# One more place in the weight ring for four of the eight expert turns

## The reference, cut to what matters

```python
def swiglu(h, w_gu, w_down):
    g, u = jnp.split(h @ w_gu, 2, axis=-1)
    return (jax.nn.silu(g) * u) @ w_down

def moe_swiglu(h, w_router, b_router, w_gu, w_down):
    tok = h.reshape(B * S, D)
    logits = tok @ w_router + b_router
    top_v, top_i = lax.top_k(logits, TOP_K)
    gates = jax.nn.softmax(top_v, axis=-1)
    combine = jnp.sum(jax.nn.one_hot(top_i, N_EXPERTS) * gates[..., None], axis=1)
    for e in range(N_EXPERTS):
        out = out + combine[:, e:e + 1] * swiglu(tok, w_gu[e], w_down[e])
    return out
```

## Time and profile before

| | |
|---|---|
| time, median of 3 runs | 1353.53 us (1351.11 to 1354.9) |
| profiled execution, its own time | 1350.77 us |
| span in the profile | 1349.0 us |
| PE, PEld busy | 96%, 75% |
| DVE, ACT busy | 63%, 48% |
| queue q1 (SP's transfers) | 393.68 MB, 76.0% of the 16 DMA engines' span |

### The profile page before, as it was taken

The page is one execution under the profiler, slowest core; times in us unless marked ns, Lnnn a source line. Parts: engine busy times, 40 slices in busy tenths (PEclk is TensorE's granted clock), DMA queues, the critical chain, the costliest instruction groups (busy, mean ns, idle before and its releaser), DMA issues.

```text
span 1349.0 us, 18058 instructions
## 1 busy us (share of the span) xinstructions
PE 1296.4 (96%) x7339; PEld 1012.9 (75%) x7339; DVE 843.6 (63%) x899; ACT 652.3 (48%) x675; POOL 86.3 (6%) x118
## 2 busy tenths in 40 slices
PE   9999999999999999999999997999979999799987
PEld 8999998888888999999888534885348863388632
DVE  6998876555555999876788304883038830388421
ACT  6545664554444454665576204762037630376401
POOL 1003000000000002100174000000000000000100
PEclk9999999999999999999999998999989999899999
DMA  9555964555554654653899999999999999999996
GB/s 314 186 194 198 337 225 162 176 189 190 188 189 143 206 188 141 218 170 123 349 403 391 386 423 424 423 422 401 423 424 423 417 385 424 424 423 419 386 423 284
DMA packets 127855, 411.89 MB, mean 305 GB/s; under 512 B 7422, under 2 KB 76382, under 8 KB 100638
## 3 DMA queue, kind: packets, MB, share of 16 engines
q1 hardware_dynamic: 121838, 393.68, 76.0%
q0 software_dynamic: 3408, 12.85, 2.5%
q10 hardware_dynamic: 2528, 4.23, 0.9%
HBM read 396.31 MB, written 14.42 MB: 304 GB/s over the span
## 4 chain that ended last, share of the span: by engine, by line
PE 83%; DMA 6%; issue 5%; ACT 3%; DVE 2%; POOL 0%; ACTq 0%; POOLq 0%; DVEq 0%; SPq 0%
PE bank L1938 23%; PE bank L1940 23%; PE bank L1939 23%; PE bank L2428 9%; DMA arena<-in_w_moe_gu 3%; DMA arena<-in_w_moe_down 2%; ACT WH L1282 1%; DVE WL L1853 1%; PE bank L2489 1%; PE bank L1982 0%; DMA xs<-in_x 0%; DMA xrows<-ysb 0%; PE bank L2359 0%; PE bank L2101 0%; PE bank L2109 0%
## 5 line engine op out<-in xcount | busy, mean ns | idle before, releaser
L1853 DVE TENSOR_TENSOR WL<-arena,WH 128x2048 fp32r<-128x2048 f32 x129 | 294.8, 2291 | 84.5 <-ACT WH L1282 84.2
L1359 DVE TENSOR_TENSOR WL<-arena,WH 128x2048 fp32r<-128x2048 f32 x108 | 245.2, 2272 | 92.8 <-ACT WH L961 92.7
L1938 PE MATMUL bank<-WH,XH 128*128 128x512 f32 (+1 forms) x728 | 274.9, 378 | 21.7 <-DVE WL L1853 21.7
L1282 ACT ACTIVATE WH<-arena 128x2048 fp32r<-128x2048 f32 x129 | 247.1, 1921 | 96.7 <-PE bank L1940 83.8
L1939 PE MATMUL bank<-WL,XH 128*128 128x512 f32 (+1 forms) x728 | 271.8, 373 | 0.0
L1940 PE MATMUL bank<-WH,XL 128*128 128x512 f32 (+1 forms) x728 | 271.1, 372 | 0.0
L961 ACT ACTIVATE WH<-arena 128x2048 fp32r<-128x2048 f32 x109 | 206.3, 1894 | 75.4 <-PE bank L1940 62.2
L1938 PEld LDWEIGHTS bank<-WH,XH 128*128 128x128 f32 x728 | 139.3, 191 | 48.7 <-DVE WL L1853 16.5
L1938 PE MATMUL bank<-XH,WH 128*128 128x256 f32 x592 | 168.1, 284 | 0.4 <-DVE XL L1389 0.4
L1940 PE MATMUL bank<-XH,WL 128*128 128x256 f32 x592 | 167.5, 283 | 0.0
L1939 PE MATMUL bank<-XL,WH 128*128 128x256 f32 x592 | 167.5, 283 | 0.0
(11 more groups left out here) (348 smaller groups left out, 1559.7 us busy)
## 6 DMA issues: line engine op xcount, KB each, us to landing
arena<-in_w_moe_gu SPq DMA_DIRECT2D x128, 1408.0 KB, 13.8
arena<-in_w_moe_down SPq DMA_DIRECT2D x84, 1024.0 KB, 16.4
arena<-in_w_in SPq DMA_DIRECT2D x27, 1024.0 KB, 5.1
arena<-in_w_ffn_gu SPq DMA_DIRECT2D x44, 512.0 KB, 4.8
arena<-in_w_xkv SPq DMA_DIRECT2D x16, 1024.0 KB, 5.3
arena<-in_w_ffn_down SPq DMA_DIRECT2D x11, 1024.0 KB, 5.0
xrows<-hTl POOLq DMA_DIRECT2D x8, 1024.0 KB, 9.1
arena<-in_w_mix_out SPq DMA_DIRECT2D x8, 1024.0 KB, 8.6
```

Of the source, the lines that this page charges most:

```text
L1282: a.activation(WH[:, (NA + i) % HL, :], raw[i % RING_M], ACT.Copy).then_inc(hi_ready, 1)
L1359: v.tensor_tensor(WL[:, n % HL, 0:w], s[:, 0:w], WH[:, n % HL, 0:w].bitcast(F32), ALU.subtract).then_inc(lo_ready, 1)
L1853: v.tensor_tensor(WL[:, (NA + i) % HL, :], raw[i % RING_M], WH[:, (NA + i) % HL, :].bitcast(F32), ALU.subtract).then_inc(lo_ready, 1)
L1938: te.matmul(out, ah, bh, start=start, stop=False, skip_group_check=shared)
```

## The change

The back half of that home, 2048 floats per partition, becomes `spare`, a twelfth unit, used in light turns alone. `early0` and `early1` move to the first third of `WH`. In a light turn the first 2048 columns of the gate lap go to `spare` and the rest to `arena` from its start; the up lap starts in `arena` unit 10, goes on in `spare` and then in `arena`; the down units 0, 1, 2 go to units 9, 10 and `spare`, the later ones to `raw[u - 3]`. Rows that cross a place's end are loaded and multiplied in pieces. `load_turn` is left with heavy turns alone.

```diff
-        WH = sb("WH", [P, HL, UNIT], F32R)
+        WH, early0, early1 = share([("WH", [P, HL, UNIT], F32R)], [("early0", [P, D], F32), ("early1", [P, D], F32)])
...
-        MH, ML, hThm, hTlm, early0, early1, hTf, xT = share(
+        MH, ML, hThm, hTlm, spare, hTf, xT = share(
             [("MH", [P, KC * S], F32R), ("ML", [P, KC * S], F32R)],
-            [("hThm", [P, D], F32R), ("hTlm", [P, D], F32R), ("early0", [P, D], F32), ("early1", [P, D], F32)],
+            [("hThm", [P, D], F32R), ("hTlm", [P, D], F32R), ("spare", [P, UNIT], F32)],
...
+        spare_landed, slot_landed = sem("spare_landed"), sem("slot_landed")
+        LIGHT_DOWN_SEM = (8, 9, 10, 0, 1, 2, 3, 4, 5, 6, 7)
+        LIGHT_DOWN_ROW = [None, 0, 1] + [(u * UNIT - 1) // FF for u in range(3, RING_M)]
...
+        def light_place(stage, c):
+            if c < UNIT:
+                return (spare, c) if stage == 0 else (arena, 10 * UNIT + c)
+            if stage == 0:
+                return arena, c - UNIT
+            return (spare, c - UNIT) if c < 2 * UNIT else (arena, c - 2 * UNIT)
...
+        def light_unit(u):
+            return spare[:, :] if u == 2 else raw[9 + u if u < 2 else u - 3]
...
+            def load_light_turn(e, turn, nth, last=False):
+                def heavy_down(u):
+                    floor = 0 if isinstance(turn, int) else LOOP_FROM // 2 * NM
+                    sp.wait_ge(lo_ready, heavy(turn, NM, max(NA - RING_M + u + 1, floor)))
+
+                load_light_row(e, 0, 0, 0, UNIT, spare_landed)
+                heavy_down(0)
+                load_light_row(e, 0, 0, UNIT, FF, part_landed[0])
+                for r in range(1, KC):
+                    heavy_down((r * FF + FF - UNIT - 1) // UNIT)
+                    load_light_row(e, 0, r, 0, FF, part_landed[r])
+                heavy_down(RING_M - 1)
+                load_light_row(e, 1, 0, 0, UNIT, slot_landed)
+                sp.wait_ge(*light_through(0, 0, nth))
+                load_light_row(e, 1, 0, UNIT, FF, part_landed[0])
+                sp.wait_ge(*light_through(0, 1, nth))
+                load_light_row(e, 1, 1, 0, 2 * UNIT - FF, part_landed[1])
+                load_light_row(e, 1, 1, 2 * UNIT - FF, FF, part_landed[1])
+                for r in range(2, KC):
+                    sp.wait_ge(*light_through(0, r, nth))
+                    load_light_row(e, 1, r, 0, FF, part_landed[r])
...
+                for u in range(RING_M):
+                    if u:
+                        sp.wait_ge(*light_through(1, LIGHT_DOWN_ROW[u], nth))
+                    load_light_down(e, u)
...
-                    if isinstance(turn, int):
-                        down_used(turn - 1, row_end(r))
...
+                    sp.wait_ge(*light_through(2, min(row_end(r) + 3, RING_M - 1), LIGHT.index(
+                        (turn if isinstance(turn, int) else LOOP_FROM) - 1)))
...
-                        pe.wait_ge(*row_in(stage, r, turn))
-                        for j, (o, w) in enumerate(SEGS):
...
+                        if r == 0:
+                            pe.wait_ge(slot_landed if stage else spare_landed, 16 * nth + 16)
+                        pe.wait_ge(*light_row_in(stage, r, turn, nth))
+                        for j, a0, w in light_pieces(stage, r):
...
-                    w = raw[u]
+                    w = light_unit(u)
```

More of the change, by code:

```diff
@@ L619, in gathered, with light_cols, light_pieces @@
             return bank[GATHER_BANK[b]][:, :].rearrange("p (c s) -> p c s", c=2)[:, :, 0:P]
+        def light_place(stage, c):
[4 more added lines that the diff above has]
+            return (spare, c - UNIT) if c < 2 * UNIT else (arena, c - 2 * UNIT)
+        def light_cols(stage, c, w):
+            tile, at = light_place(stage, c)
+            last_tile, last = light_place(stage, c + w - 1)
+            assert tile is last_tile and last == at + w - 1
+            return tile[:, at:at + w]
+        def light_unit(u):
+            return spare[:, :] if u == 2 else raw[9 + u if u < 2 else u - 3]
+        def light_pieces(stage, r):
+            pieces = []
+            for j, (o, w) in enumerate(SEGS):
+                cuts = {0, w}
+                for start in (r * FF + o, r * FF + FF // 2 + o):
+                    for edge in ((UNIT,), (UNIT, 2 * UNIT))[stage]:
+                        if start < edge < start + w:
+                            cuts.add(edge - start)
+                cuts = sorted(cuts)
+                pieces += [(j, a, b - a) for a, b in zip(cuts, cuts[1:])]
+            return pieces
         def heavy_sg(j):
@@ L668, in load_row, with load_down, load_light_row @@
                 sp.dma_start(arena[:, r * FF:r * FF + FF], src).then_inc(part_landed[r], 16)
-            def load_down(e, u, light):
+            def load_down(e, u):
+                src = w_moe_down[0][bass.ds(e, 1), u * 256:u * 256 + 256].rearrange("o (p k) n -> (o p) (k n)", k=2)
+                sp.dma_start(raw[u], src).then_inc(part_landed[DOWN_SEM[u]], 16)
+            def load_light_row(e, stage, r, c0, c1, landed):
+                w = w_moe_gu[0].rearrange("e (k p) (s f) -> e k s p f", p=P, s=2)
+                src = w[bass.ds(e, 1), r, stage, :, c0:c1].rearrange("o p f -> (o p) f")
+                sp.dma_start(light_cols(stage, r * FF + c0, c1 - c0), src).then_inc(landed, 16)
@@ L671, in load_down, with load_light_down @@
+            def load_light_down(e, u):
                 half = FF // 2
-                if light and u == 10:
-                    for k, landed in enumerate((part_landed[DOWN_SEM[u]], last_half)):
+                if u == 10:
+                    for k, landed in enumerate((part_landed[LIGHT_DOWN_SEM[u]], last_half)):
                         src = w_moe_down[0][bass.ds(e, 1), half * k + half - P:half * k + half]
-                        sp.dma_start(raw[u][:, k * D:k * D + D], src.rearrange("o p n -> (o p) n")).then_inc(landed, 16)
+                        sp.dma_start(light_unit(u)[:, k * D:k * D + D], src.rearrange("o p n -> (o p) n")
+                                     ).then_inc(landed, 16)
@@ L676, in load_down @@
                     return
-                f0 = u // 5 * half + u % 5 * 256 if light else u * 256
+                f0 = u // 5 * half + u % 5 * 256
                 src = w_moe_down[0][bass.ds(e, 1), f0:f0 + 256].rearrange("o (p k) n -> (o p) (k n)", k=2)
-                sp.dma_start(raw[u], src).then_inc(part_landed[DOWN_SEM[u]], 16)
+                sp.dma_start(light_unit(u), src).then_inc(part_landed[LIGHT_DOWN_SEM[u]], 16)
+            def load_light_turn(e, turn, nth, last=False):
[18 more added lines that the diff above has]
+                    load_light_row(e, 1, r, 0, FF, part_landed[r])
+                    if r == 4 and not last:
+                        load_rows(turn + 1, turn, rows_of(turn + 1))
+                for u in range(RING_M):
+                    if u:
+                        sp.wait_ge(*light_through(1, LIGHT_DOWN_ROW[u], nth))
+                    load_light_down(e, u)
@@ L681, in row_end, with load_turn @@
             def row_end(r):
                 return (r * FF + FF - 1) // UNIT
[L684 to L690, removed]
+            def load_turn(e, turn, gate_rows=True):
                 for r in range(KC):
@@ L693, in load_turn @@
                         continue
-                    if isinstance(turn, int):
-                        down_used(turn - 1, row_end(r))
-                    else:
-                        if not last:
-                            sp.wait_ge(*light_through(2, row_end(r), LIGHT.index(LOOP_FROM - 1)))
+                    sp.wait_ge(*light_through(2, min(row_end(r) + 3, RING_M - 1), LIGHT.index(
+                        (turn if isinstance(turn, int) else LOOP_FROM) - 1)))
+                    if not isinstance(turn, int):
                         sp.wait_ge(lo_ready, heavy(turn, NM, max(NA - RING_M + row_end(r) + 1, LOOP_FROM // 2 * NM)))
@@ L701, in load_turn @@
                 for r in range(KC):
[L702 to L705, removed]
+                    sp.wait_ge(lo_ready, heavy(turn, NM, NA + row_end(r) + 1))
                     load_row(e, 1, r)
-                    if r == 4 and gate_rows and not last:
+                    if r == 4 and gate_rows:
                         load_rows(turn + 1, turn, rows_of(turn + 1))
                 for u in range(RING_M):
[L710 to L714, removed]
+                    sp.wait_ge(lo_ready, heavy(turn, NM, NA + RING_M + u + 1))
+                    load_down(e, u)
             last_dense = {i: max(n for n in range(NA) if n % RING_A == i) for i in range(RING_A)}
@@ L743, in _ @@
             for turn in range(1, LOOP_FROM):
-                load_turn(expert_at(turn + 1), turn, LIGHT.index(turn) if turn in LIGHT else None)
+                if turn in LIGHT:
+                    load_light_turn(expert_at(turn + 1), turn, LIGHT.index(turn))
+                else:
+                    load_turn(expert_at(turn + 1), turn)
```

(34 more changed lines are left out.)

## The result

Medians of six runs each, in turn on the same chip: 1342.74 us with the change (1341.84 to 1343.69), 1352.38 before (1350.3 to 1354.9). The ratio of the two on record is 0.9936, 95% interval 0.9924 to 0.9948: 8.7 us faster, 7.0 to 10.3. (The two medians lie 9.6 us apart, inside that interval.) Forecast were 4.9 us and 1348.6, with a range whose low end was 1344.5. Timed again later, against the kernel before, the same kernel gave 0.9944 (0.9931 to 0.9957), 7.6 us. The direction was right, the size was not.

What follows compares the result with a forecast made beforehand. The prediction took the expert part as bound by the weight stream, with dips left to gain. Stands of 6.7 us less 1.8 for transfers gave 4.9 us: 1353.5 to 1348.6 us, range 1344.5 to 1354.0.

Steps and rivals of the forecast that it cites:

- The wait for the heavy gate row: After each light turn PE still waits for the stream, 24.10 us from issue to landing, so gains are kept.
- the cost term: Twelve further transfers, three per light turn, each 0.15 us of fixed time on the stream: 1.8 us.
- the sum of the stands: Idle stream time saved around the ends of heavy turns, over turns 1, 3, 5 and 7: 6.7 us.
- the landings: Turn 3's saving from landing times: up row 1 at 939.0 against 941.0, so 2.0 us.
- the bytes: Turn 3's saving from bytes moved: the stretch 924.2 to 937.6 at 386 GB/s against 424, so 1.2 us.
- The sum of the high ends: Upper savings of turns 3, 5, 1 and 7 added: 2.0 + 2.1 + 1.6 + 2.5 = 8.2 us.
- the dry point: End of a heavy turn, where the queue is nearly drained; 2.5 us more of work would lie there.
- PE's further products: Six more products per light turn, at most 2.4 us each turn, hidden behind PE's waits for down units.
- The late heavy gate rows (C): Rival: heavy gate rows, waiting for light down units three later, come late; 7 us slower, 1361; chance 0.04.
- A, dips that are work: Rival: the stream's dips are mostly work, not idle; gain 3.4 - 1.8 = 1.6 us, 1351.9; chance 0.22.
- D, the whole loss: Rival: earlier releases recover the whole slow stretches, 11.0 less 1.8, 9.2 us, 1344.3; chance 0.07.
- The rule of 2.0 us per transfer: Skill's fixed time per transfer; as stream time 12 pieces cost 24 us; judged latency a filled queue hides.

Runs made afterwards that it cites:

- e2: The changed kernel with each light-turn transfer waiting as long as before, places and pieces kept: 1350.56 us, ratio 1.0 to the kernel before.
- e1: The kernel before with every gate and up row loaded in two transfers of 1408 columns, 128 more: 1352.18 us against 1350.98, ratio 1.0009.
- e3: The changed kernel with the first 2048 columns of up row 0 waiting as before, gate rows still early: 1346.55 us, ratio 0.9963 to the kernel before.
- e7: The changed kernel with a thirteenth place, the third part of WL, in light turns: 1340.34 us against 1343.02, ratio 0.9925 to the kernel before.

## Why the prediction was right or wrong

*What bounds it.* Right. The expert part is the weight stream; what fell off the time were its stands at the end of heavy turns, and e2 shows that nothing but the earlier issue does it. The wait for the heavy gate row stayed after each light turn, and the four gains added up. What failed are sizes: of the 3.2 us between the forecast 4.9 and the 8.1 of the table, 1.8 are the cost term and 1.4 the sum of the stands.

*What it costs.* The step that failed is the term "12 x 0.15 = 1.8 us". It came from the difference between 427 and 420 GB/s of two stretches, laid to a fixed time per transfer. In e1 a further transfer costs 0.06 to 0.08 us of the running stream, half of that, and 0.01 us of the whole time; e2, with all twelve pieces, shows no cost within 2 us. Two stretches of different rows, 1.7% apart, could not price a piece, and what a piece costs the stream need not show in the time (why it didn't in e1 is argued above, not shown).

*The sum of the stands.* 6.7 us, measured 8.1 (1.5, 2.4, 1.8, 2.4 by the table against 1.6, 1.6, 1.9, 1.6). That turns 1 and 5 agree to 0.1 us is luck, since a single turn is good to about 1 us. For turn 3 the landings had said 2.0 and the bytes 1.2, and I took 1.6; the measured 2.4 lies nearer to the landings. For turn 7 I took 1.6 between 0.9 and 2.5; 1.1 to 2.4 was measured. The sum of the high ends, 2.0 + 2.1 + 1.6 + 2.5 = 8.2, is what came out, so taking less than it was the second error of size. It is not a proof of that count: the bytes under the same caps make 1.2 + 1.8 + 1.6 + 2.5 = 7.1, which the times (7.6 and 8.7, each within some 1.7) don't tell from it. Both counts look only at the rows around the dry point, and e3 shows that the rows ahead of it lose time too.

*The range.* Its end of 1344.5 was 1353.5 less the high end of 8.2 and a bit. With six runs the kernel before has 1352.4. That 1.1 us of the base, and no room below the high end for it, put 1342.7 outside.

*PE's further products.* Hidden, as said: e2 has them all and shows no cost within 2 us.

*The late heavy gate rows (C).* Nothing within 2 us: e2 keeps them and stands at before, and e7, with four units, is faster still.

*A, dips that are work.* Wrong: nearly the whole 8.2 us of the high ends came, where A allowed 3.4. The dips alone would not settle it, as e1 and the second trace of turn 7 show.

*D, the whole loss.* Not with this change: turn 1 kept 371 GB/s. e7, with a further place and an earlier release, takes 2.7 us more, most of what is left of D's 11.0.

*The rule of 2.0 us per transfer.* The weighing held: in the running stream a further transfer costs 0.06 to 0.08 us (e1), so the 2.0 us are not time of the stream. The Trainium skill (DMA: Bandwidth & Descriptors, Anatomy of one DMA) has that fit from transfers issued by POOL, which the prediction did not say; those here are issued by SP.

## What to carry to other kernels

Where a stream is paced by the places that a slower consumer frees, a further place is worth the time for which the stream stands, up to the transfer time of that place per stand; read the stand from landing to landing, and look at what the first release behind it lets go. Don't take the GB/s of one stretch as proof of a gain: here a kernel with fuller stretches (e1) was no faster. Cutting rows of 1.4 MB in two cost 0.06 to 0.08 us per piece in the running stream and nearly nothing in the time, probably because this stream had stands to take it up. A small difference between two bandwidths is no measure of a cost per transfer: double the number of transfers of the same rows, time it, and read its stream too.

## What was not expected of the hardware

Loading 128 rows of 1408 KB as 256 transfers of 704 KB cost 1.2 us in 1352 (e1), within the error of nothing, though the full stream fell from 427 to 419 GB/s. A row issued at the same point of the cycle landed 8.0 us after its issue in one kernel and 9.3 in another, with the same bytes issued in total, when the rows ahead of it had been issued some 3 us earlier (e3); the cause is open.
